# A fused attention-and-pooling block on Trainium2: x^T laid out by the host, 1/rms applied after the projection, and ten products of ones at the start

## The reference

```python
h = rms_norm(x, norm_w)                     # x: 512 x 2048, rms over 2048
proj = h @ w_in                             # w_in: 2048 x 6144
q, k, v, g_a, u_p, g_p = jnp.split(proj, [A, 2*A, 3*A, 4*A, 4*A + P], axis=-1)   # A = P = 1024
attn = diff_attention(q, k, v, ...)         # q, k: rms_norm over 64, rope, two softmaxes per head
pool = multiscale_pool(u_p, w_pool, pool_scale)
mixed = concatenate([attn * silu(g_a), pool * silu(g_p)])
return x + mixed @ w_out                    # w_out: 2048 x 2048
```

## Time and profile before

| what | value |
|---|---|
| median of 3 runs | 803.97 us (802.61 to 804.04) |
| the profiled execution | 802.5 us, its span 800.7 us |
| TensorE busy | 780.2 us, 97% |
| VectorE busy | 530.8 us, 66% |
| ScalarE busy | 402.8 us, 50% |
| GpSimd busy | 30.4 us, 4% |
| bytes moved | 101.75 MB, mean 127 GB/s |

### The profile page before, as it was taken

One profiled execution on the slowest core, in us unless ns is written; L12 is line 12 of the kernel. 1 busy time (PEld: TensorE's weight loads), 2 busy tenths in 40 slices (PEclk: granted clock), 3 DMA queues, 4 the chain that ended last, 5 costly groups with the idle time before them and its releaser, 6 DMA issues.

```text
span 800.7 us, 10143 instructions
## 1 busy us (share of the span) xinstructions
PE 780.2 (97%) x3520; PEld 645.1 (81%) x3520; DVE 530.8 (66%) x794; ACT 402.8 (50%) x654; POOL 30.4 (4%) x37
## 2 busy tenths in 40 slices
PE   3899999999999999999999999999999999999998
PEld 3688888888888888888888888888888888888886
DVE  5728766763486667626856675277666788777796
ACT  6644445543554456433646444444455466555552
POOL 1000000000000000000000000000000020233100
PEclk9999999999999999999999999999999999999999
DMA  9333622223236222232442222326222489999912
GB/s 343 90 106 105 177 78 68 74 79 105 79 110 174 61 74 79 79 105 81 138 126 75 79 79 78 105 96 167 78 79 79 157 226 295 338 255 211 199 53 105
DMA packets 67096, 101.75 MB, mean 127 GB/s; under 512 B 4865, under 2 KB 54273, under 8 KB 66561
## 3 DMA queue, kind: packets, MB, share of 16 engines
q1 hardware_dynamic: 60592, 82.52, 32.2%
q0 software_dynamic: 4608, 16.78, 10.6%
q10 hardware_dynamic: 1874, 2.18, 1.0%
HBM read 90.98 MB, written 4.19 MB: 119 GB/s over the span
## 4 chain that ended last, share of the span: by engine, by line
PE 96%; DVE 2%; ACT 1%; DMA 1%; issue 0%; DVEq 0%; ACTq 0%
PE ps L392 94%; PE ps L482 2%; DVE mixed L794 1%; DVE h_lo L784 1%; DMA mixed<-in_x 1%; ACT at_hi L570 0%; PE ps L454 0%; PE ps L384 0%; ACT h_hi L563 0%; DVE x_left L1021 0%; ACT x_rms L573 0%; DVE x_rstd L793 0%; DVEq L792 0%; ACTq L568 0%
## 5 line engine op out<-in xcount | busy, mean ns | idle before, releaser
L392 PE MATMUL ps<-h_hi,w_hi 128*128 128x512 f32 x768 | 302.2, 394 | 1.3 <-DVE h_lo L784 1.3
L392 PE MATMUL ps<-h_lo,w_hi 128*128 128x512 f32 x768 | 299.5, 390 | 0.0
L800 DVE TENSOR_TENSOR w_lo<-raw,w_hi 128x512 fp32r<-128x512 f32 x192 | 131.2, 690 | 191.2 <-ACT w_hi L585 188.6
L585 ACT CAST w_hi<-raw 128x512 fp32r<-128x512 f32 x192 | 118.8, 622 | 249.2 <-PE ps L392 248.2
L392 PE MATMUL ps<-h_hi,w_lo 128*128 128x512 f32 x768 | 205.8, 390 | 0.0
L392 PEld LDWEIGHTS ps<-h_hi,w_hi 128*128 128x128 f32 x768 | 144.3, 188 | 31.1 <-issue 1.6
L392 PEld LDWEIGHTS ps<-h_hi,w_lo 128*128 128x128 f32 x768 | 144.2, 188 | 30.5
L392 PEld LDWEIGHTS ps<-h_lo,w_hi 128*128 128x128 f32 x768 | 144.4, 188 | 29.3
L392 PE MATMUL ps<-w_hi,h_lo 128*128 128x512 f32 x224 | 87.2, 389 | 0.0
L392 PE MATMUL ps<-w_hi,h_hi 128*128 128x512 f32 x224 | 87.2, 389 | 0.0
L392 PE MATMUL ps<-w_lo,h_hi 128*128 128x512 f32 x224 | 87.2, 389 | 0.0
(11 more groups left out here) (129 smaller groups left out, 797.0 us busy)
## 6 DMA issues: line engine op xcount, KB each, us to landing
raw<-in_w_in SPq DMA_DIRECT2D x96, 512.0 KB, 3.6
tall<-in_w_out SPq DMA_DIRECT2D x16, 512.0 KB, 12.0
raw<-in_w_out POOLq DMA_DIRECT2D x12, 512.0 KB, 11.7
wide_b<-in_w_out POOLq DMA_DIRECT2D x12, 512.0 KB, 14.6
mixed<-in_x SPq DMA_DIRECT2D x4, 1024.0 KB, 8.4
tall<-in_w_out POOLq DMA_DIRECT2D x8, 512.0 KB, 14.0
kh_twice<-kh_twice SPq DMA_DIRECT2D x8, 256.0 KB, 5.2
kl_twice<-kl_twice SPq DMA_DIRECT2D x8, 256.0 KB, 5.9
```

The lines of the kernel that those rows point to most:

```text
L392: last = nc.tensor.matmul(dst, lhs, rhs, start=first and i == 0, stop=final and i == len(pairs) - 1, skip_group_check=True)
L585: nc.scalar.copy(w_hi[:, h % W_SLOTS, :], raw[:, unit % RAW_SLOTS, part * 512:part * 512 + 512]).then_inc(w_hi_ready, 1)
L800: nc.vector.tensor_tensor(w_lo[:, h % W_SLOTS, :], raw[:, unit % RAW_SLOTS, part * 512:part * 512 + 512], w_hi[:, h % W_SLOTS, :].bitcast( ...
```

## The change

The host passes x a second time, transposed (`x_cols`), and norm_w as a 128 x 16 tile. h^T is now x^T times norm_w per partition, without 1/rms: ScalarE and VectorE read it from SBUF. 1/rms goes to the columns of the results: for V, GA, U and GP VectorE multiplies by `rstd_row` as it takes them out of PSUM, and Silu is applied by ScalarE afterwards in SBUF. Q and K are normed anyway; only their epsilon has to be scaled by mean(x^2), so a row of that (`eps_row`) is added to their sums of squares by VectorE. The row sums of x come from a second load of x in rows, taken by ScalarE at m = 5 to 8 of round 0. One product of ones with a diagonal tile spreads the epsilons over the partitions; GpSimd spreads 1/rms. The first halves of round 0 have their loads, high and low parts mixed with those of x^T. Round 0 is written out ahead of the loop. Ten products of a tile of ones go into a bank that is overwritten later, at the start.

```diff
 @block.sync
-            for t in range(ST):
-                sp.dma_start(x_rows[:, t, :], x_tiles[:, t, :]).then_inc(x_in[t], 16)
...
-            for unit in range(RAW_SLOTS):
-                load_in(unit, 0)
+            load_x_cols(0, 0, 2)
+            load_in(0, 0)
+            load_x_cols(1, 2, 4)
+            load_x_cols(2, 4, 8)
+            load_in(1, 0)
+            load_x_cols(3, 8, 12)
+            load_in(2, 0)
+            load_x_cols(4, 12, 16)
+            load_in(3, 0)
             for dst, src in ((ones_pair[:, :], pair_ones), (cos_t[:, :], rope_cos),
...
                 sp.dma_start(lam_in[:, n, :], src.to_broadcast([P, HEAD_DIM])).then_inc(lam_loaded, 16)
+            load_x_row(0)
+            load_x_row(1)
 @block.gpsimd
+            nc.gpsimd.memset(ones_f32, 1.0).then_inc(ones_set, 1)
+            pool.wait_ge(x_rstd_ready, 1)
+            for t in range(ST):
+                pool.dma_start(rstd_line[:, t * P:(t + 1) * P], x_rstd[:, t:t + 1]).then_inc(rstd_line_in, 16)
+            pool.wait_ge(rstd_line_in, 16 * ST)
+            nc.gpsimd.partition_broadcast(rstd_row[:, :], rstd_line, P).then_inc(rstd_spread, 1)
 @block.tensor
-            for t in range(ST):
-                pe.wait_ge(x_normed, t + 1)
...
+            pe.wait_ge(ones_set, 1)
+            for n in range(WARM):                       # WARM = 10
+                nc.tensor.matmul(ps[:, OB, 0:P], ones_f32, ones_f32, start=True, stop=True)
...
+                    if first and g == K:
+                        pe.wait_ge(h_lo_ready, hk + 1)
...
+                    if first and m == 9:
+                        pe.wait_ge(eps_diag_ready, ST)
+                        nc.tensor.matmul(ps[:, OB, :], ones_f32, eps_diag, start=True, stop=True).then_inc(eps_spread, 1)
                     if m in (9, 17):
...
 @block.scalar
+            def x_high(q):
+                act.wait_ge(x_in[q if q < 2 else 1 + q // 2], 16)
+                for kk in range(2):
+                    k = 2 * q + kk
+                    nc.scalar.activation(h_hi[:, k, :], x_turned[:, k, :], ACT.Copy,
+                                         scale=nw[:, k:k + 1]).then_inc(h_hi_ready, 1)
...
+                if t == ST - 1:                          # in x_stats(t)
+                    act.wait_ge(x_squared, ST)
+                    nc.scalar.activation(x_rms[:, :], x_ss[:, :], ACT.Sqrt, bias=eps_t[:, :],
...
+            for q in range(4):
+                x_high(q)
+                split_high(q, 0)
...
+                    if first and m <= 4:
+                        x_high(m + 3)
...
                         if n == 0:                       # m == 8
                             nc.scalar.preload_act_table_set(LN_EXP)
+                        if first and n == 0:
+                            act.wait_ge(lam_summed, 1)
+                            nc.scalar.activation(lam_exp[:, :], lam_sum[:, :], ACT.Exp).then_inc(lam_exped, 1)
...
-                        rstd(wk(3 * n), ps[:, S0:S0 + 2, :], HEAD_DIM, r * 4 + n + 1)
+                        act.wait_ge(sums_raised, r * 2 + n + 1)
+                        log_exp(wk(3 * n), wk(2), HEAD_DIM, 0.0, r * 4 + n + 1)
...
                         split_high(m + 3, r)
+                    if first and m in (1, 2):
+                        act.dma_start(x_rows[:, m + 1, :], x_tiles[:, m + 1, :]).then_inc(x_row_in[m + 1], 16)
+                    if first and 5 <= m <= 8:
+                        x_stats(m - 5)
...
-                        nc.scalar.copy(wk(4), ps[:, 0:2, :]).then_inc(evacuated, 1)
...
-                        nc.scalar.activation(gate[:, :, :], ps[:, 2:4, :], ACT.Silu).then_inc(evacuated, 1)
+                        act.wait_ge(evacuated, r * 4 + 2 + START)
+                        nc.scalar.activation(gate[:, :, :], gate[:, :, :], ACT.Silu).then_inc(gate_ready, 1)
...
 @block.vector
+                    k = 2 * q + kk                        # in x_low(q)
+                    dve.wait_ge(h_hi_ready, k + 1)
+                    ins = nc.vector.scalar_tensor_tensor(
+                        out=h_lo[:, k, :], in0=x_turned[:, k, :], scalar=nw[:, k:k + 1],
+                        in1=h_hi[:, k, :].bitcast(F32), op0=ALU.mult, op1=ALU.subtract)
...
+                    if first and m == 9:
+                        dve.wait_ge(x_squared, ST)
+                        setup(nc.vector.tensor_scalar(x_eps[:, :], x_ss[:, :], HEAD_DIM * EPS / D,
+                                                      HEAD_DIM * EPS * EPS, ALU.mult, ALU.add))
+                        for t in range(ST):
+                            nc.vector.tensor_scalar(eps_diag[:, t * P:(t + 1) * P], ident[:, :], x_eps[:, t:t + 1],
+                                                    None, ALU.mult).then_inc(eps_diag_ready, 1)
+                    if first and m == 9:
+                        dve.wait_ge(x_rms_ready, 1)
+                        nc.vector.reciprocal(x_rstd[:, :], x_rms[:, :]).then_inc(x_rstd_ready, 1)
+                    if first and m == 10:
+                        dve.wait_ge(eps_spread, 1)
+                        nc.vector.tensor_copy(eps_row[:, :], ps[:, OB, :]).then_inc(eps_row_ready, 1)
+                        dve.wait_ge(eps_row_ready, 1)
+                    if m == 18:
+                        qk_low(0, 0)
+                    if m in (10, 18):
...
+                        nc.vector.tensor_tensor(wk(2), ps[:, S0:S0 + 2, :], twice(eps_row), ALU.add
+                                                ).then_inc(sums_raised, 1)
...
+                    if m == 24:
+                        if first:
+                            dve.wait_ge(rstd_spread, 1)
+                        dve.wait_ge(w_used, r * HALVES + 24)
+                        scale_evac(wk(4), V).then_inc(evacuated, 1)
+                    if m == 33:
+                        dve.wait_ge(w_used, r * HALVES + 32)
+                        scale_evac(gate[:, :, :], GA).then_inc(evacuated, 1)
+                    if m == 40:
+                        dve.wait_ge(w_used, r * HALVES + 40)
+                        scale_evac(wk(0), U).then_inc(evacuated, 1)
...
+                        dve.wait_ge(w_used, r * HALVES + HALVES)      # m == 48
+                        scale_evac(wk(0), GP).then_inc(evacuated, 1)
```

More of the change, by code:

```diff
@@ L519, in _ @@
                         last.then_inc(pool_done, 1)
+            pe_round(0, first=True)
+            with pe.Fori(1, ROUNDS) as r:
+                pe_round(r)
             pe.wait_ge(evacuated, ROUNDS * 4 - 1 + START)
@@ L848, in chain, with qk_low @@
                     dve.wait_ge(dve_step, r * STEPS + step[0])
-                for m in range(1, HALVES + 1):
+                def qk_low(n, c):
+                    rows = slice(64 * c, 64 * c + 64)
+                    dve.wait_ge(qk_hi_ready, r * 4 + 2 * n + c + 1)
+                    nc.vector.tensor_tensor(q_low[rows] if n else kl_twice[rows, c], wk(0)[rows],
+                                            (kh_twice, q_stack)[n][rows, c].bitcast(F32), ALU.subtract
+                                            ).then_inc((k_low_ready, q_low_ready)[n], 1)
@@ L889, in dve_round @@
                         n = int(m == 22)
-                        for c in range(2):
-                            rows = slice(64 * c, 64 * c + 64)
-                            dve.wait_ge(qk_hi_ready, r * 4 + 2 * n + c + 1)
-                            nc.vector.tensor_tensor(q_low[rows] if n else kl_twice[rows, c], wk(0)[rows],
-                                                    (kh_twice, q_stack)[n][rows, c].bitcast(F32), ALU.subtract
-                                                    ).then_inc((k_low_ready, q_low_ready)[n], 1)
+                        for c in range(1 - n, 2):
+                            qk_low(n, c)
                     i, odd = divmod(m - 25, 2)
@@ L984, in dve_round @@
                 assert step[0] == STEPS, step[0]
-            with dve.Fori(0, ROUNDS - 1) as r:
+            dve_round(0, first=True)
+            with dve.Fori(1, ROUNDS - 1) as r:
                 dve_round(r)
@@ L1070 @@
 CONSTS = 8
+WARM = 10
 LN_EXP = "natural_log_exp_and_others"
```

195 lines of the change are left out of this document (81 added, 114 removed).

## The result

The changed kernel takes 814.93 us (median of 4 runs, 814.77 to 815.6) against 804.0 us for the one before (802.61 to 804.25): ratio 1.0141, 95% interval 1.0124 to 1.0159. The profiled execution has a span of 813.7 us against 800.7. The forecast was 806.8 us with a range to 811.5: the direction was right, the size was not, and the time lies outside the range.

What follows compares the result with a forecast made beforehand. TensorE, busy 97% and without a gap from 28.18 us, bounds the kernel, so only the start and new waits count. Half 10 earlier (-2.4) plus q-path waits (+5.2) give +2.8 us: 806.8 us on the median, range 801.0 to 811.5.

Steps and rivals of the forecast that it cites:

- The first product at 8.3 us: Start of round 0: TensorE's first projection product comes at about 8.3 us in place of 28.18 us.
- The start isn't what sets half 10: Round 0: a start up to 3 us later than 8.3 us would change nothing.
- The weights of half 8: Fifth weight transfer, SyncE's queue: lands at 34.9 us (31.5 to 38.5), so TensorE stands still from 30.1 to about 35.6.
- ScalarE's order: ScalarE, round 0, m = 5 to 8: row sums, copies, table load and squares take 14.0 us, ending at 48.9 us.
- Half 10 19.1 us behind the landing: Round 0: after row sums, eps_diag and low squares, half 10 starts at 54.0 us against 56.43, 2.4 us won.
- rival 3: TensorE, half 10 of round 0: runs at half clock, 2.7 us more, so 809.5; chance 0.10.
- The q path: Every round, before the scores: two added VectorE operations delay q by 1.8 us, slack 0.5, wait 1.3; four rounds 5.2 us.
- Rival 1: q path before the scores: more slack than read, so only the start counts, 801.6; chance 0.17.
- The drain of a table load: ScalarE's two table loads before half 10: the skill's 1.38 us drain would add 2.8 us, forecast 809.6; left out.
- The rest at nothing: Each round: four evacuations moved from ScalarE to VectorE (1.22 us each) and GpSimd's 1/rms row cost nothing.
- Rival 2: Start of round 0: x's second load doesn't hold back the weights; 16 us won, 5.2 given back, 793.2; chance 0.08.
- Rival 4: Prologue: another wait, for instance ScalarE held issuing two x tiles into full queues, 1 to 4 us, about 809.5; chance 0.10.

Runs made afterwards that it cites:

- the control: The changed kernel run again, unaltered, on the same chip; 815.10 us.
- The run with 8 columns: Changed kernel with the sums of squares of x's rows taken over 8 of the 2048 columns, all transfers and waits kept; 807.02 us.
- the run with the one load: Changed kernel with one load of the logarithm and exponential table set put behind the first round's square root; 807.98 us.
- the change with its side costs mended: Changed kernel with packed constants, the table set loaded once and the shorter q path, without reordering loads or row sums; 800.35 us.

## Why the prediction was wrong

- *The bound of the kernel* (TensorE without a gap, so new waits and the start alone count): right. 12.8 of the 13.0 us are found in waits and in the clock.
- *The first product at 8.3 us*: 7.71 us. *The start isn't what sets half 10*: right, by the run without the ten products.
- *The weights of half 8 at 34.9 us, bounds 31.5 to 38.5*: **this is the step that failed.** They landed at 41.65 us (40.2 in the control), outside the bounds. The sum took every byte at a rate that large rows had shown, and counted the constants by their 0.72 MB. Nine of these transfers are small pieces and hold up what is behind them by about 1.0 MB, in either queue, with the engines largely idle. Packed, the copy starts at 36.47 us, 3.7 to 5.2 us earlier, 1.5 us behind the forecast and inside its bounds; this last 1.5 us stays unexplained. The kernel before has the same transfers, but no weights wait behind them there. Its windows show them, the last landing at about 24 us:

```profile
20.00:22.00 2.00, 1.07 (x8) 0.83 (x8) 1.96 (x3) 2.00 (x4) 0.00 (x0) 1.00 0.45 91
22.00:24.00 2.00, 0.43 (x2) 0.44 (x3) 2.00 (x2) 2.00 (x4) 0.00 (x0) 0.73 0.08 19
```

With nothing else in the queue they take some 4 us. The forecast took its rates from ahead of 18 us and nothing from here.
- *ScalarE's order, 14.0 us from landing to the last row sum*: right in mechanism and nearly in size, 13.1 us (a row sum and the copy behind it take 2.4 us, not 2.64). The run with 8 columns confirms it, at 7.9 us for the sums.
- *Half 10 19.1 us behind the landing*: 18.0 us. With the landing 6.75 us late and this 1.1 us short, half 10 is at 59.63 us instead of 54.0. Five and a half of the ten missing microseconds are here.
- *The clock at half 10*, rival 3: it was true as well, at 1.1 us instead of 2.7, since TensorE works from 55.94 us on and the clock comes back at about 62.1 us. It had been given a chance of its own, as if it were an alternative to the forecast. It goes with every late landing and belonged into the sum.
- *The q path, 1.3 us of stall in each of four rounds*: right for rounds 1 to 3 (1.37, 1.38, 1.14), in part because two small errors cancel: 1.6 us longer instead of 1.8, and 0.25 us of slack instead of 0.5. Rival 1, more slack, falls. In the first round it is 2.5 us and the lower clock behind it adds 1.65 us. Missed there: a table load between logarithm and exponential. The row sums' square root stands behind the preload of the other set, so the logarithm and the exponential each load again. ScalarE, first round, q:

```profile
85.63 1.06 ACT L618 ACTIVATE work<-work 128x1024 f32<-128x1024 f32 x1 [1.72 <-DVE work L886]
86.71 1.28 ACT L620 ACT_TABLE_LOAD   x1
88.00 1.06 ACT L620 ACTIVATE work<-work 128x1024 f32<-128x1024 f32 x1
```

- *The drain of a table load*: not seen. The exponential of the lambdas starts at 50.33 us, 1.29 us after the load at 49.04; here the exponential follows 1.29 us after its load. The forecast was right to leave it out; the time by it would have been nearer, for another reason.
- *The rest at nothing*: 0.4 to 0.5 us in the output stage, otherwise right.
- *Rival 2*, the second load of x holds nothing back: falls by the run without it, 13.2 us. *Rival 4*, another wait of the longer prologue: in a way the hole is one, but the instance it names isn't: ScalarE issued its two tiles of x in 0.36 us each.

The missing 10 us are therefore 6.75 - 1.1 us of landing and order, 1.1 us of clock at half 10, 2.9 us of table load and clock in the first round (2.53 - 1.3 + 1.65; in the run with the one load both are gone, but its time mixes them with the earlier landing), and 0.5 us in the output stage.

## What to carry to other kernels

Whoever takes work off the start should write down what every transfer in the queue costs in time and not in bytes: here nine transfers of 4 or 256 bytes a row held up the queue as long as 1 MB would have, the cost moved with them to another queue, and one packed array took it away. A gain at the start is worth only what the next late thing leaves of it; here that was the same data loaded a second time ahead of the weights; a version that also moves it and the row sums behind them, and reorders the squares and the epsilon product with them, took 789.86 us, against 800.35 for the change with its side costs mended. A stall of TensorE of 2.5 us cost another 1.65 us in clock, while the stalls of 1.4 us cost none here, so among waits of the same kind the longest is mended first.

## What the runs showed that I had not expected

- Nine transfers of together 0.13 MB hold up the others by about 2.7 us, in SyncE's queue at 26 to 32 us as in GpSimd's at 8 to 20 us, and this is no work of the engines: they are busy for 0.38 and 0.46 of the time from 28 to 32 us.
- Ten products of ones, 2.8 us of idleness, and then the clock is at half all the same; 18 of them, with 0.9 us between, and the first half runs at full clock. That there was work before does not suffice, then; whether the shorter gap or the longer work decides isn't separated.
- A landing time of the same transfers that differs between kernels by 1.7 to 4.3 us (37.37 and 38.41 us against 40.14 to 41.67 in seven others), with its cause left open.
